# Routing stage of a two-layer mixture of experts: one scaling operation, squares added in pairs on GpSimd, tokens moved by VectorE

## The reference, cut to what matters

```python
def modulate(x, g, shift, scale):
    return rmsnorm(x, g) * (1 + scale) + shift
...
    x = x + gt_m * y
    hf = modulate(x, norm_ffn[i], sh_f, sc_f).reshape(b * s, d)
...
    pg = jax.nn.softmax(hf @ router_g.astype(f32), axis=-1)
    gi = jnp.argmax(pg, axis=-1).astype(jnp.int32)
    le = (hf @ router_e.astype(f32)).reshape(t, N_GROUPS, EXPERTS_PER_GROUP)
    le_sel = jnp.take_along_axis(le, gi[:, None, None], axis=1)[:, 0]
    pk, ik = lax.top_k(jax.nn.softmax(le_sel, axis=-1), TOP_K)
    wts = pg_sel * pk / jnp.sum(pk, axis=-1, keepdims=True)
```

## Time and profile before

| | us |
|---|---|
| median of three runs | 2576.7 |
| lowest and highest run | 2573.59, 2577.34 |
| the profiled execution's own time | 2581.72 |
| its span | 2579.3 |
| mean granted TensorE clock in it | 0.928 |

### The profile page before, as it was taken

The page is one execution under the profiler, slowest core; times in us unless marked ns, Lnnn a source line. Parts: engine busy times, 40 slices in busy tenths (PEclk is TensorE's granted clock), DMA queues, the critical chain, the costliest instruction groups (busy, mean ns, idle before and its releaser), DMA issues. The chain is left out here.

```text
span 2579.3 us, 26865 instructions
## 1 busy us (share of the span) xinstructions
PE 2301.4 (89%) x11316; PEld 1524.4 (59%) x11316; DVE 631.7 (24%) x1455; ACT 477.9 (19%) x889; POOL 196.1 (8%) x256
## 2 busy tenths in 40 slices
PE   6999696876999699888998899999979689999997
PEld 5755385565888575567877544454448554544453
DVE  2556112012220223562221211111110221111112
ACT  1222401111220233533331100000011120000000
POOL 2023001001111112310001000000000100000000
PEclk9999697998999789997887999999989889999998
DMA  5469542222443111010006699999954369999993
GB/s 192 163 247 332 211 172 82 98 75 89 139 155 105 65 66 65 34 46 20 1 2 246 289 427 428 427 426 427 427 193 163 134 267 427 426 428 427 427 427 148
DMA packets 120019, 575.55 MB, mean 223 GB/s; under 512 B 5152, under 2 KB 28281, under 8 KB 95321
## 3 DMA queue, kind: packets, MB, share of 16 engines
q1 hardware_dynamic: 118431, 570.59, 55.6%
q0 software_dynamic: 768, 2.02, 0.4%
q10 hardware_dynamic: 698, 1.18, 0.2%
HBM read 572.72 MB, written 1.05 MB: 222 GB/s over the span
## 5 line engine op out<-in xcount | busy, mean ns | idle before, releaser
L426 PE MATMUL linear_ps<-hT,ring 128*128 128x256 f32 x1344 | 300.3, 387 | 39.0 <-PEq L345 18.3
L426 PEld LDWEIGHTS linear_ps<-hT,ring 128*128 128x128 f32 x1344 | 260.6, 194 | 78.4 <-issue 41.7
L2485 PE MATMUL ex_u<-ring_extra,ex_xt 128*64 128x512 f32 x1024 | 224.3, 592 | 3.0 <-DMA ring_extra<-in_w 3.0
L2485 PE MATMUL ex_u<-ring,ex_xt 128*64 128x512 f32 x1024 | 223.9, 592 | 1.5 <-issue 1.5
L1651 PE MATMUL dl_front<-dn_src,ring 128*128 128x256 f32 (+1 forms) x512 | 177.4, 503 | 2.0 <-DVE dp_cv L1818 2.0
L2485 PEld LDWEIGHTS ex_u<-ring_extra,ex_xt 128*64 128x64 f32 x1024 | 74.9, 137 | 148.7 <-issue 148.7
L2485 PEld LDWEIGHTS ex_u<-ring,ex_xt 128*64 128x64 f32 x1024 | 75.2, 137 | 145.1 <-issue 145.1
L1113 PE MATMUL ffn_ps<-hT,ring 128*128 128x256 f32 x704 | 155.2, 384 | 5.9 <-PEq L345 5.9
L1113 PEld LDWEIGHTS ffn_ps<-hT,ring 128*128 128x128 f32 x704 | 135.8, 193 | 25.3 <-issue 6.3
L2574 DVE TENSOR_TENSOR ex_hid<-ex_sil,ex_u 128x512 f32<-128x512 f32 x32 | 34.6, 1082 | 425.3 <-PE ex_u L2485 425.3
L1651 PEld LDWEIGHTS dl_front<-dn_src,ring 128*128 128x128 f32 x512 | 99.3, 199 | 65.8 <-issue 58.9
(11 more groups left out here) (493 smaller groups left out, 2775.1 us busy)
## 6 DMA issues: line engine op xcount, KB each, us to landing
ring<-in_w SPq DMA_DIRECT2D x96, 2048.0 KB, 19.0
ring_extra<-in_w SPq DMA_DIRECT2D x96, 2048.0 KB, 20.7
ring<-in_ada_w SPq DMA_DIRECT2D x24, 2048.0 KB, 8.4
ring<-in_ffn_w_up SPq DMA_DIRECT2D x22, 1024.0 KB, 6.5
ring<-in_w_in SPq DMA_DIRECT2D x8, 2048.0 KB, 8.8
ring<-in_w_in_a SPq DMA_DIRECT2D x8, 2048.0 KB, 8.2
ring<-in_w_in_b SPq DMA_DIRECT2D x6, 2048.0 KB, 20.7
ring<-in_ffn_w_down SPq DMA_DIRECT2D x5, 2048.0 KB, 8.8
```

The costliest lines, as they stand in the source:

```text
L426: mm = pe.matmul(ps[:, q % banks, 0:n], w[:, k, j * P:(j + 1) * P], src[:, k, 0:n], start=k == 0, stop=k == kc - 1)
L2485: mm = pe.matmul(u[H * a:H * a + H, i, :], xt[:, b, k, H * a:H * a + H], w[a][:, 512 * k:512 * k + 512], start=k == 0, stop=k == KC - 1, s ...
```

## The change

GpSimd scales all eight column blocks in one tensor_tensor, with the gains broadcast along the 36 columns; TensorE's logits wait for that one operation. GpSimd also adds the squared blocks in pairs: after two of ScalarE's four operations it adds blocks 2 and 3 onto 0 and 1, after all four blocks 6 and 7 onto 4 and 5. TensorE then sums four blocks instead of eight, which makes 8 products where there were 16. The eight `s_ps` products move from between the quads to ahead of the logits. The counts move to between the third and the fourth quad.

The quads leave PSUM on VectorE: one scalar_tensor_tensor for each multiplies by the inverted root, adds the shift and writes the token rows, so that ScalarE's four moves and GpSimd's two additions of the shift go away. These four operations stand behind L2335 on VectorE and ahead of the weights, and wait first for both halves of `srow`. ScalarE keeps its two moves of `srow`, right behind the eight scaled copies.

```diff
-            for k in range(KC):
-                pool.tensor_scalar(rg[:, k, :], rw[:, k, :], gain(k), None, ALU.mult).then_inc(weighed.sem, weighed.tick())
+            pool.tensor_tensor(rg[:, :, :], rw, gains.unsqueeze(2).broadcast_to([P, KC, NG]), ALU.mult).then_inc(weighed.sem, weighed.tick())
...
-            for t in range(TT):
-                pool.wait_ge(moved.sem, moved.at(2 * (t + 1)))
-                pool.wait_ge(rowed.sem, rowed.at(3))
-                pool.tensor_tensor(R["tokens"][:, t, :], R["tokens"][:, t, :], srow[:, :], ALU.add).then_inc(shifted.sem, shifted.tick())
+            for q in (0, 1):
+                pool.wait_ge(squared.sem, squared.at(2 * q + 2))
+                pool.tensor_tensor(wide(2 * q), wide(2 * q), wide(2 * q + 1), ALU.add).then_inc(shifted.sem, shifted.tick())
...
-            for q, (a, c) in enumerate(quads):
-                act.wait_ge(turned.sem, turned.at(q + 1))
-                if q == 0:
-                    act.wait_ge(inverted.sem, inverted.at(1))
-                act.activation(by_row(R["tokens"][:, a, :], c), t_ps[:, q % 2, :].rearrange("t (q k) -> t k q", k=KC), ACT.Copy,
-                               scale=root[:, a:a + 1]).then_inc(moved.sem, moved.tick())
...
+            dve.wait_ge(rowed.sem, rowed.at(3))
+            for q, (a, c) in enumerate(quads):
+                dve.wait_ge(turned.sem, turned.at(q + 1))
+                dve.scalar_tensor_tensor(out=by_row(R["tokens"][:, a, :], c), in0=t_ps[:, q % 2, :].rearrange("t (q k) -> t k q", k=KC),
+                                         scalar=root[:, a:a + 1], in1=by_row(srow[:, :], c), op0=ALU.mult,
+                                         op1=ALU.add).then_inc(moved.sem, moved.tick())
             dve.wait_ge(exps.sem, exps.at(2))
```

More of the change, by code:

```diff
@@ L2147, in _, with stage_moe_head @@
                 dve.tensor_tensor(dst[:, c, :], cv[:, c, :], proj[:, c, :], ALU.mult)
-def stage_moe_head(K, l, y, gate, gain, shift, R):
+def stage_moe_head(K, l, y, gate, gains, shift, R):
     nc = K.nc
@@ L2164, in stage_moe_head @@
         rw = K.routers[:, l]
+        gain = lambda k: gains[:, k:k + 1]
         rg = K.sb("rt_rg", [P, KC, NG], ctx=st)
@@ L2218, in _ @@
             mm.then_inc(biased.sem, biased.tick())
+            for q in range(2):
+                for j in range(4):
+                    mm = pe.matmul(s_ps[:, q, j * P:(j + 1) * P], shift(4 * q + j).broadcast_to([P, P]), K.ident[:, :],
+                                   start=True, stop=True)
+                mm.then_inc(moved_bias.sem, moved_bias.tick())
             for t in range(TT):
@@ L2226, in _ @@
             mm.then_inc(full.sem, full.tick())
+            sums = (0, 1, 4, 5)
             for t in range(TT):
-                for k in range(KC):
-                    if t == 0 and k % 2 == 0:
-                        pe.wait_ge(squared.sem, squared.at(k // 2 + 1))
-                    mm = pe.matmul(n_ps[:, t:t + 1], sq[:, k, t * P:(t + 1) * P], K.ones[:, 0:1], start=k == 0, stop=k == KC - 1)
+                for k in sums:
+                    if t == 0 and k % 4 == 0:
+                        pe.wait_ge(shifted.sem, shifted.at(k // 4 + 1))
+                    mm = pe.matmul(n_ps[:, t:t + 1], sq[:, k, t * P:(t + 1) * P], K.ones[:, 0:1], start=k == 0, stop=k == sums[-1])
             mm.then_inc(sized.sem, sized.tick())
             for q, (a, c) in enumerate(quads):
+                if q == 3:
+                    pe.wait_ge(chosen.sem, chosen.at(1))
+                    pe.matmul(c_ps[:, 0:N_EXP], K.incl[:, 0, :], hot[:, 0, 2, :], start=True, stop=True)
+                    pe.matmul(c_ps[:, N_EXP:2 * N_EXP], K.incl[:, 0, :], hot[:, 1, 2, :], start=True, stop=False)
+                    pe.matmul(c_ps[:, N_EXP:2 * N_EXP], K.ones[:, :], hot[:, 0, 2, :], start=False, stop=True)
+                    pe.matmul(c_ps[:, 2 * N_EXP:3 * N_EXP], K.ones[:, :], hot[:, 0, 2, :], start=True, stop=False)
+                    pe.matmul(c_ps[:, 2 * N_EXP:3 * N_EXP], K.ones[:, :], hot[:, 1, 2, :], start=False,
+                              stop=True).then_inc(counted.sem, counted.tick())
                 if q >= 2:
@@ L2788, in second_block @@
             K.extra_slots(slots)
[L2789 removed]
+            stage_moe_head(K, 0, K.hT, mod(0, 0, 2), K.gains[0][:, 0, 1, :], mod(0, 0, 3), R)
             stage_experts(K, 0, R, mod(0, 0, 5))
```

29 lines of the change are left out of this document (9 added, 20 removed).

## The result

The changed kernel took 2562.0 us at the median of 20 runs, the kernel before 2577.5 at the median of 20. The ratio is 0.9938, 95% interval 0.9918 to 0.9958: faster by 15.4 us at the medians, by 10.8 to 21 by the interval. Two more series of the changed kernel gave 0.9944 (0.9917 to 0.9971) and 0.9955 (0.993 to 0.9981), that is 13.1 and 12.7 us at the medians. The forecast was 2568.7, 8.0 us, with a range that ended at 2563.0. The direction was right, the size was not: the gain was nearly twice the forecast. The first series missed the range by 1.0 us, less than its scatter, and the other two, with 13.1 and 12.7 us, lie inside the range's 13.7.

The account below looks back on a forecast made before the run. TensorE, busy for 89% of the span, was taken to set the routing fronts, with routing on the path. Fronts 6.1 plus tails 1.9 made 8.0 us, off 2576.7: 2568.7 us, range 2563 to 2575.5.

Parts of the forecast that it names:

- Bounds and stages: Whole kernel: TensorE busy 89% of the span, the routing stage on the path in both layers, gain kept through the experts.
- Rival D: Experts' weight transfers take the whole gain: 2576.7 us, chance 6%.
- Front, GpSimd: Routing front: one scaling of 0.8 us and pair sums of 1.05 to 1.2 us cost nothing.
- Front of layer 0: Layer 0's routing, first instruction to square root: 4.15 us earlier than 15.45.
- (a): Routing front, clock full until the logits are done, then low: 11.3 us, 4.15 earlier than 15.45.
- Front of layer 1: Layer 1's routing, first instruction to square root: 1.95 us gained, the middle of (a) and (c).
- (c): Routing front, clock low from 2 us in: 16.2 us, 0.5 later than layer 1's 15.7.
- Tail: Routing stage, square root to VectorE's last operation: 0.95 us earlier per layer, 1.9 in all.
- M: Price of each of VectorE's four moves out of PSUM in the tail: 0.75 us taken, ends 0.75 and 1.08.
- R: Start of the square root, where the tail begins; the tail was to end at R + 13.8 us against R + 14.75.
- The two pages: Tail: transposes do not count as busy, so the clock stays low; a PSUM line penalty puts M nearer 1.08 us.
- C: Rival: the clock also holds or rises in the tail, 14.5 us earlier, 2562.2 us; chance 8%.

Follow-up runs that it names:

- before: The kernel before the change, unchanged: 2577.5 us at the median.
- after2: The changed kernel as it is, recorded a second time: 2563.7 us, ratio 0.9944 to the kernel before.
- after3: The changed kernel as it is, recorded once more: 2564.7 us, ratio 0.9955 to the kernel before.
- rg8: The changed kernel with the router's columns scaled in eight operations as before: 2565.2 us, one run.
- pad8: The changed kernel with eight more one-column products on TensorE behind the last quad, awaited by nobody: 2568.4 us, ratio 0.9948 to the kernel before.
- act_move: The changed kernel with tokens moved by ScalarE and the shift added by GpSimd again: 2563.9 us, ratio 0.9952 to the kernel before.
- counts_last: The changed kernel with the counts behind the fourth quad, measured twice: 2564.2 and 2549.4 us, ratios 0.9931 and 0.9918 to the kernel before.
- cl_pad4: counts_last with four more one-column products behind the counts, awaited by nobody: 2566.4 us, one run.
- only_srow: The kernel before with only the eight shift products moved ahead of the logits: 2579.5 us, ratio 0.9995 to the kernel before.
- before2: The kernel before, unchanged, traced a second time: 2581.8 us, ratio 1.0003.
- srow_late: The changed kernel with the eight shift products back between the quads: 2568.4 us, ratio 0.9975 to the kernel before.
- sums16: The changed kernel without GpSimd's pair sums, TensorE summing all eight squared blocks: 2574.3 us, ratio 1.0 to the kernel before.

## Why the prediction was wrong in size, step by step

In layer 0's front and in both tails the mechanism was the forecast one. What failed are three terms of the sum. Layer 1's front was put at 1.95 us and measured 3.8, because the clock took a course that was not on the list. The tails were put at 0.95 each and measured 1.8, and layer 0's front at 4.15 and measured 5.1; in both, durations had been added end to end where the rows overlap, and the tail of layer 1 before was taken from layer 0.

**Bounds and stages: right.** The gain lies in the front and the tail of the two routing stages, and the experts took it over almost whole: from the gather's first product to VectorE's last addition layer 0 takes 466.5 us in before, 466.4 in after2 and 467.3 in after3, and the weights are waited for 2.8 us in both layers together, 3.0 in before. Rival D is out.

**Front, GpSimd: right.** The scaling took 0.67 us (0.8 taken), the pair sums 1.57 and 1.27 (1.05 to 1.2 taken, a little short). VectorE's adds are held, 4.71 us for 3.26, less than the 5.2 taken. No one waited. Were rg at its upper end of 4.7, the forecast had 0.8 us a layer of cost; rg8 shows that even then there is none.

**Front of layer 0: (a) was right, its size short.** The clock fell 7.7 us in, with the logits done. The step took 11.3 us; seven of the eight traces with this front on TensorE (after2, after3, act_move, rg8, pad8, both of counts_last, cl_pad4) have 9.76 to 10.19, one 12.56. Two things make the difference of 1.1 to 1.5 us. I added durations of rows end to end, but at full clock the rows overlap: 1396.66, 1398.43, 1400.30 and 1403.80 are 1.77, 1.87 and 3.50 apart where I had put 1.95, 1.95 and 3.90. And the sums had their first pieces at full clock, 3.01 us for 3.48. Mean of the eight: 10.3, a gain of 5.1 and not 4.15.

**Front of layer 1: the step that failed most.** I listed four courses, full and then low, and low from some point to the end, and took the middle of (a) and (c), −1.95. The one that happens was not on the list: the clock is low when the stage starts or soon after, and comes **back** while the shift products run. In after2 it is low until 6.3 us in, high to 9.7, low again; the slice from 2052 to 2054 above shows it at 0.77 and the one from 2056 at 0.68. The 32 pieces of the logits last:

```profile
2053.27 4.08 PE L2231 MATMUL rt_ps<-rt_rg,xT 128*128 128x36 f32 x32
2057.15 3.55 PE L2239 MATMUL rt_sizes<-ones,rt_sq 128*128 128x1 f32 x16
```

Eight traces with this order have 10.7 to 14.1 us, mean 12.7, against 15.7 and 17.2 of before: a gain of 3.8 and not 1.95, and 1.6 in the one trace of after2. The return belongs to the shift products: it came while they ran in all eight and in only_srow, and the three traces without them there (before, before2, srow_late), once low, stay low to 18.7 us or later. sums16 alone has them and no return. Yet in this front they no more than pay for themselves: srow_late, with 16 pieces fewer, has 12.31. What is gained in it is nearly all the halved sums, 16 pieces of 0.218 or 3.5 us. That was in the forecast; what failed is the clock's course, for which (c), half of the middle, had the shift products cost 1.9 us more than at full clock and the logits 3.1 more. after3 shows the return in numbers, clock 0.50 at first, 1.00 from 2058 to 2061:

```profile
2055.00:2057.00 2.00, 2.00 (x12) 2.00 (x10) 2.00 (x3) 0.82 (x2) 1.57 (x1) 0.50 0.98 418
2058.00:2061.00 3.00, 3.00 (x29) 3.00 (x28) 0.00 (x0) 0.00 (x0) 1.12 (x1) 1.00 0.99 426
```

**Tail: right in its chain, 0.7 and 1.0 us short in its size.** The order of events is the one forecast: two moves, a third, a wait for the turn behind the counts, 0.16 us for L2341. M is 0.748 us (eight operations), the value taken. But the last move ended at R + 10.5 and not R + 11.0: the counts hold the turn back for 2.0 us and not 2.2, and turns overlap what stands ahead of them, again from adding durations end to end. The end at R + 13.1 instead of R + 13.8 makes 1.6 us in layer 0; in layer 1 before had 15.1 where I used layer 0's 14.75 for both, which makes 2.0. The two traces of before have 14.75 to 15.13, so the gain is 1.8 on the average instead of 0.95. Not foreseen was its inner split: by only_srow and counts_last it is 1.5 to 1.7 us for s_ps out of the tail and 2.1 for VectorE's moves, less 2.0 for the early counts.

**The two pages.** The clock stayed low through the tail, from 1404.4 to 1424.9, as by the rule that transposes do not count as busy (the Trainium skill, TensorE: Matmul & The Clock Gate, Part 4: PE-mode transpose). That the level was right does not show the rule, and only_srow speaks against it: in layer 0 its clock went from 0.50 to 1.00 behind transposes alone, with one pause of 0.49 us among them. In the changed kernel's tail they come four at a time, 1.11 us each, with 0.5 and 1.1 us of idle between. Whether that idle time keeps the clock low there was not tested. srow_late, with the wide products mixed into the transposes again, had it at 1.00 between 1413.6 and 1417.0, 18 to 21 us in, as before had it up again 21 us in. By the penalty on PSUM elements that do not share a line (the Trainium skill, Advanced Engine Details and Errata, Memory Cachelines) M would have been nearer 1.08. The page names matmuls as what slows down, and the prediction carried it over to VectorE. M is 0.75, the same as an operation with plain reading, so for VectorE this trace does not bear it out.

**The sum.** With the means of the eight traces the terms are 5.1 + 3.8 + 1.8 + 1.8 = 12.5 us in place of 8.0, and the exits give up to 3 or take 1. That fits the 12.7 and 13.1 us of the two later series and lies in the interval of the first. Two terms that the sum put at nothing nearly cancel: the first gather, "the gather's own time stays", takes 6.1 to 7.2 us in after2, after3, rg8 and pad8 (mean 6.6) and 6.15 to 6.34 in before and before2, since more of it runs at the low clock, which is 0.8 us lost over both layers; the exits are 1.4 us shorter on the average. The two traces of the changed kernel itself show less, 9.3 to 11 us in the rest; both are executions at the slow end of their series (2568.2 and 2571.1 us). What is left, up to 3 us of the 15.4 of the first series, I can't assign: the scatter of the delta stage is larger than that.

**The rivals.** C gave 2562.2, next to the measured 2562.0, but its mechanism did not occur: the tail's clock stayed low. That the measured time stands next to C's is luck: the number was met by other terms. The range ended at 2563.0, "just short of C", and so took the forecast's own unknowns as smaller than they were: the front of layer 1 alone spans 3.4 us between executions of the same order.

## What to carry to other kernels

Work that must be done anyway and is wide can be placed where TensorE has only thin products: sixteen pieces more in layer 0's front came with a front that was 2.3 us shorter (only_srow against before, 2.1 against before2). In layer 1's, where the clock fell sooner, the same order brought nothing by itself. A small operation put ahead of a hand-over between engines pays only if its own result is wanted first; the counts' was not, and it cost 2 us in each layer. In a sum for pipelined TensorE rows, take the distance between starts and not the durations, and read each layer's own figures. Where runs fall into groups, compare within a group before believing a median.

## What the hardware showed beyond that

- The granted clock, once low, can come back in the middle of a front: in the eight traces of the changed front, layer 1 went from 0.50 to 1.00 between 4.7 and 6.3 us into the stage, and in one of them layer 0 too. In sums16 it did not, with the same products there. In before, before2 and srow_late, without them, it came back 18.0 us in at the earliest.
- It can also rise behind transposes alone: 0.50 to 1.00 at 18.5 us into layer 0 of only_srow, in one trace.
- A branch over a skipped block costs TensorE 0.4 to 0.5 us or 3.3 to 5.9 us (L2637 in after2: 5.88 in layer 0, 0.36 in layer 1), by how many instructions stand ahead of it; sixteen pieces more in each layer (pad8) turn one case into the other at both exits, eight (cl_pad4) at the second alone. That it is the fetching of instructions is argued, not shown.
- The delta stage, unchanged in all of them, takes 180.8 or 191.7 to 198.3 us by the clock it is granted, and so the same program's time moves by some 15 us from one execution to the next. Twelve runs a side tell 7 us apart, not 3.
- GpSimd and VectorE slow each other down, but not with every operation. VectorE's eight adds take 3.26 us beside GpSimd's eight tensor_scalar in before and in rg8, 3.70 in sums16 beside the one tensor_tensor, and 4.71 with the pair sums too. The pair sum beside them takes 1.57 us and the one after them 1.27; in rg8, where both come later, the two take 2.48.
